# Differential attention in a two-layer diffusion backbone: units of two heads against units of one head with alternating score banks

## Chip, cores and metric

The program runs on one core of a Trainium2 chip, as one launch. The metric is the device time of that launch in microseconds (us).

## What is computed

Two layers over 256 latent tokens (x) and 256 context tokens, model width 1024, all in float32. Layer 0 mixes tokens by a Fourier transform and windowed attention and ends in a dense SwiGLU. Layer 1 has the differential attention that this case is about, and then a SwiGLU over 8 experts of which each token takes two. The reference, cut to the differential attention:

```python
def diff_attend(q, k, v, lam):                 # 8 heads, 2 maps c per head, d = 64, v has e = 128
    s = jnp.einsum('bqhcd,bkhcd->bhcqk', q, k).astype(jnp.float32) * (q.shape[-1] ** -0.5)
    p = jax.nn.softmax(s, axis=-1)
    w = p[:, :, 0] - lam * p[:, :, 1]
    return jnp.einsum('bhqk,bkhe->bqhe', w.astype(v.dtype), v)

# diff_mixer: keys and values are those of context and x together (512); queries those of x (2 tiles of 128)
ox = (rmsnorm(ox, subln_g) * (1.0 - lam_init)).reshape(B, L, D_MODEL) @ w_out
```

So a head has two softmax maps over the same 512 keys, the second is subtracted with a factor, and the output of each head (128 wide) is normalised by its own root mean square before the output projection.

## The kernel before

The code is written engine by engine, each engine's program in one function, with counting semaphores between them; every engine works strictly in the order of its own program. The sync queue (SP) loads weights, the POOL queue loads small tables and the rows of the modulation.

**Weights.** Until the experts, weights come in blocks of 1 MB into a ring of six slots (`WRAW`, line 127), in the order of `raw_order` (lines 389 to 394); a slot is refilled when its block of six places before has been used (lines 449 to 461). There are two kinds. A modulation block (`ada`, line 961) is multiplied straight from the slot, four matrix products into bank 7, 8 blocks to a group of rows; `ada_rows` (line 1503) adds the bias on VectorE once a group is complete, and POOL stores the rows (`store`, line 541). A projection block is split into a high part on ScalarE (`hi_upto`, line 613) and a low part on VectorE (`lo_upto`, line 1475), into rings of `SPL` = 3 buffers; the low part releases the slot. The output projection of the second attention has four such blocks, `B_DOUT` and the next three. In `raw_order` the modulation blocks 32 to 47, which belong to the time of this attention, are mixed with them: blocks 32 to 43, two output blocks, 44 to 47, two output blocks.

**Second attention.** PSUM has 8 banks of 128x512. Work goes in 8 groups g of one query tile t = g // 4 and two heads, so four score maps. Per group:

- TensorE, lines 1242 to 1265: two modulation blocks; the scores of group g+1, four products into banks 0 to 3 (`scores1`, line 1225), as soon as ScalarE has read the banks; then, when VectorE has combined the maps of g, eight transposes of 128x128 into banks 4 and 5; then, when ScalarE has copied these out, eight products with the values into bank 6.
- ScalarE, lines 825 to 848: copies banks 4 and 5 out to `PT1`; the exponentials of group g+1 (`exps1`, line 815), four instructions, each of which also sums its rows into `SUMS`; then copies the outputs from bank 6 and squares them with sums for the later normalisation.
- VectorE, lines 1745 to 1765: waits for the exponentials; reciprocal of the sums, times lambda, scales the two first maps, adds the two second maps scaled (`P1`); then the row maximum of group g+1 over banks 0 to 3 and its negation (`maxima1`, line 1732).

Three other jobs stand in these loops. At g = 5 VectorE normalises query tile 0 (`sub_norm`, line 1737), for which ScalarE takes a square root (line 846). At g = 3 and 7 VectorE adds the modulation rows (line 1759). At g = 6 and 7 output blocks 0 and 1 are split, ScalarE's part behind its squares (line 848), VectorE's behind its maximum (line 1762). Behind the loop come the normalisation of tile 1, the transposes of the output (line 1271), their high parts on ScalarE (line 853), the low part of output block 2 (line 1768) and the low parts of the output (line 1771), and then the output projection (line 1275).

**What follows.** SP loads the first expert blocks once all scores are issued (line 497) and their places are free. POOL waits for the last value product (line 598), then loads gate and norm rows. The expert stage (`experts`, line 1344) runs over 8 experts with a ring of 14 slots of 1 MB; SP refills a slot when TensorE has used it.

Of the kernel before, what the change touches and what calls it, by code (L numbers as in the profile page):

```python
# [75 lines left out]
SPLIT_AHEAD = 2  # L76
ADA_ATT0 = [3, 3, 2, 2, 2, 2, 2, 0]
# [39 lines left out]
def backbone(nc, x, c, ctx_in, c_ctx, ada_w, ada_b, norm_g, mix_in_w, mix_out_w, win_sink, diff_qkv_w,  # L117
# [111 lines left out]

    TRI, ROPE = T2[:, 0:256], T2[:, 256:448]  # L230
# [212 lines left out]
    def _(sp):  # L443
# [51 lines left out]
        def experts(rnd):  # L495
            if rnd == 0:
                sp.wait_ge(scores, 16)
# [35 lines left out]
    def _(pool):  # L533
# [49 lines left out]
        pool.wait_ge(pv_done, 8)  # L583
# [14 lines left out]
        pool.wait_ge(pv_done, 16)  # L598
# [11 lines left out]
    def _(act):  # L610
# [204 lines left out]
        def exps1(g):  # L815
            act.wait_ge(negmax, 8 + g + 1)
            if g:
                act.wait_ge(p_tr, 24 + 2 * g)
            for j in range(4):
                ins = act.activation(P1[:, j, :], ps[:, j, :], ACT.Exp, bias=NEGM[:, j:j + 1], scale=SCALE,  # L820
                                     accum_out=SUMS[:, j:j + 1])
            ins.then_inc(exps, 1)

        exps1(0)
        for g in range(8):
            t, hp = g // 4, g % 4
            act.wait_ge(p_tr, 24 + 2 * g + 1)
            act.wait_ge(pv_done, 8 + g)
            act.activation(PT1[:, 0:2, :], ps[:, 4, :].rearrange("p (c q) -> p c q", c=2),
                           ACT.Copy).then_inc(pt_even, 1)  # L830
            act.wait_ge(p_tr, 24 + 2 * g + 2)
            act.activation(PT1[:, 2:4, :], ps[:, 5, :].rearrange("p (c q) -> p c q", c=2),
                           ACT.Copy).then_inc(pt_odd, 1)
            if g < 7:
                exps1(g + 1)
            act.wait_ge(pv_done, 8 + g + 1)
            act.activation(OA[:, t, 256 * hp:256 * hp + 256], ps[:, 6, 0:256], ACT.Copy)
            if g:
                act.wait_ge(o_raw, g)
            for hh in range(2):  # L840
                n_ = t * 8 + 2 * hp + hh
                ins = act.activation(T2[:, P * hh:P * hh + P], ps[:, 6, P * hh:P * hh + P], ACT.Square,
                                     accum_out=SS[:, n_:n_ + 1])
            ins.then_inc(o_raw, 1)
            if g == 5:
                sqrt(0, 8)
            if g >= 6:
                hi_upto(B_DOUT + g - 5)
# [99 lines left out]
    def _(pe):  # L948
# [276 lines left out]
        def scores1(g):  # L1225

            t, hp = g // 4, g % 4
            if g:
                pe.wait_ge(exps, 8 + g)
            else:  # L1230
# [744 lines left out]
```

## Time and profile before

| | before |
|---|---|
| median of 3 runs | 1974.8 us (1969.48 to 1976.64) |
| profiled execution, its own time | 1977.56 us |
| span of the profile | 1975.8 us |
| TensorE matmuls busy | 1820.3 us (92%) |
| VectorE, ScalarE busy | 475.0 us (24%), 386.9 us (20%) |
| mean granted clock of TensorE | 0.952 of full |

A matmul in float32 is recorded as two instructions, so eight products show as x16. Almost all of TensorE's products are issued through one helper and so carry line 950; what they are is read from their operands: `work` alone are scores, `work,pt` are values, `w_raw,cond_stationary` are modulation blocks. Times in a timeline are microseconds from the span's start.

### The profile page before, as it was taken

How to read it: one execution, taken by the hardware profiler on the slowest of the kernel's cores; microseconds unless marked ns; L12 is line 12 of the kernel's file. 1: busy time of each engine (PE TensorE's matmuls, PEld its weight loads, DVE VectorE, ACT ScalarE, POOL GpSimd, SP SyncE). 2: the span in 40 equal slices, each digit the busy share in tenths (PEclk: the TensorE clock that was granted, in tenths of full speed). 3: DMA queues.
4: the chain of work that ended last, by engine and by line, in shares of the span. 5: the costliest groups of instructions: out<-in, count | busy, mean ns of one | idle time of the engine just before them, and what ended most of it. 6: DMA issues, size and time to landing. Idle time of an engine off the chain costs nothing. (4 is left out here: it accounts for less than half of the span.)

```text
span 1975.8 us, 35831 instructions
## 1 busy us (share of the span) xinstructions
PE 1820.3 (92%) x16214; PEld 1069.0 (54%) x16214; DVE 475.0 (24%) x762; ACT 386.9 (20%) x662; POOL 34.8 (2%) x71
## 2 busy tenths in 40 slices
PE   5999789999999889865799999999999999999995
PEld 2743478888888768544535345353443534435342
DVE  3313445222233663454310100101001010010103
ACT  3223433222232432342100000100001000010001
POOL 1000100000000000000000000000000000000000
PEclk8998899999999999987699999999999999999997
DMA  9255462332324232347599999999999999999970
GB/s 372 96 171 171 144 187 72 99 100 93 107 86 138 69 109 84 129 150 271 228 339 367 369 363 375 327 364 373 368 361 335 364 371 361 368 334 365 369 294 24
DMA packets 141160, 477.43 MB, mean 242 GB/s; under 512 B 11168, under 2 KB 35096, under 8 KB 122576
## 3 DMA queue, kind: packets, MB, share of 16 engines
q1 hardware_dynamic: 137344, 467.64, 64.5%
q0 software_dynamic: 3664, 7.48, 1.2%
q8 instruction: 129, 2.11, 0.4%
q14 instruction: 23, 0.19, 0.0%
HBM read 473.96 MB, written 1.13 MB: 240 GB/s over the span
## 5 line engine op out<-in xcount | busy, mean ns | idle before, releaser
L950 PE MATMUL ps<-w_hi,h_t 128*128 128x512 f32 (+1 forms) x960 | 298.2, 391 | 18.9 <-DVE h_t L1532 7.2
L950 PE MATMUL ps<-w_moe,h_te 128*32 128x256 f32 (+1 forms) x3520 | 296.6, 493 | 16.4 <-DVE residual L1876 16.4
L950 PE MATMUL ps<-h_t,w_hi 128*128 128x512 f32 (+1 forms) x768 | 222.5, 374 | 5.0 <-DVE h_t L1532 5.0
L950 PEld LDWEIGHTS ps<-w_moe,h_te 128*32 128x32 f32 x3520 | 113.2, 111 | 193.3 <-issue 138.9
L950 PE MATMUL ps<-w_raw,h_te 128*32 128x256 f32 (+2 forms) x3648 | 216.8, 396 | 0.0
L1479 DVE TENSOR_TENSOR w_lo<-w_raw,w_hi 128x2048 fp32r<-128x2048 f32 x58 | 132.9, 2292 | 349.0 <-ACT w_hi L619 348.5
L950 PEld LDWEIGHTS ps<-w_hi,h_t 128*128 128x128 f32 x960 | 182.6, 193 | 59.7 <-issue 8.3
L950 PE MATMUL ps<-w_lo,h_t 128*128 128x512 f32 (+1 forms) x480 | 186.9, 389 | 0.0
L1875 DVE TENSOR_TENSOR residual<-silu_g,ps 128x512 f32<-128x512 f32 (+1 forms) x32 | 19.8, 618 | 650.7 <-ACT silu_g L894 650.7
L619 ACT ACTIVATE w_hi<-w_raw 128x2048 fp32r<-128x2048 f32 x58 | 110.8, 1914 | 327.9 <-PE ps L950 319.4
L950 PEld LDWEIGHTS ps<-w_raw,h_te 128*32 128x32 f32 x3648 | 112.2, 110 | 100.9 <-issue 61.5
L950 PE MATMUL ps<-w_raw,work 128*32 128x512 f32 x1984 | 166.2, 487 | 0.0
L950 PEld LDWEIGHTS ps<-h_t,w_hi 128*128 128x128 f32 x768 | 141.9, 191 | 30.3 <-issue 5.6
L893 ACT ACTIVATE silu_g<-ps 128x512 f32<-128x512 f32 (+1 forms) x32 | 17.4, 544 | 655.1 <-PE ps L950 655.1
L950 PE MATMUL ps<-work 128*32 128x256 f32 (+6 forms) x752 | 137.7, 521 | 7.9 <-ACT p L820 4.9
L950 PE MATMUL ps<-h_t,w_lo 128*128 128x512 f32 (+1 forms) x384 | 143.6, 374 | 0.0
L950 PEld LDWEIGHTS ps<-w_raw,work 128*32 128x32 f32 x1984 | 62.0, 110 | 96.2 <-issue 77.1
L950 PEld LDWEIGHTS ps<-w_lo,h_t 128*128 128x128 f32 x480 | 92.7, 193 | 17.8
L950 PEld LDWEIGHTS ps<-work 128*32 128x32 f32 (+3 forms) x752 | 51.5, 135 | 75.1 <-issue 46.4
L950 PE MATMUL ps<-w_moe,work 128*32 128x512 f32 (+1 forms) x1088 | 91.0, 487 | 0.0
L950 PE MATMUL ps<-work,h_te 128*32 128x256 f32 (+1 forms) x1024 | 88.7, 493 | 1.0 <-ACT h_te L882 1.0
L950 PEld LDWEIGHTS ps<-h_t,w_lo 128*128 128x128 f32 x384 | 73.4, 191 | 12.6
(233 smaller groups left out, 1213.6 us busy)
## 6 DMA issues: line engine op xcount, KB each, us to landing
w_moe<-in_expert_in_w_dram SPq DMA_DIRECT2D x110, 1024.0 KB, 6.2
w_raw<-in_expert_out_w_dram SPq DMA_DIRECT2D x62, 1024.0 KB, 7.1
w_raw<-in_expert_in_w_dram SPq DMA_DIRECT2D x50, 1024.0 KB, 7.7
w_raw<-in_ada_w_dram SPq DMA_DIRECT2D x48, 1024.0 KB, 5.0
w_moe<-in_expert_out_w_dram SPq DMA_DIRECT2D x34, 1024.0 KB, 7.0
work<-in_expert_in_w_dram SPq DMA_DIRECT2D x32, 1024.0 KB, 7.2
w_raw<-in_expert_in_w_dram SPq DMA_DIRECT2D x64, 512.0 KB, 4.8
w_raw<-in_ffn_in_w_dram SPq DMA_DIRECT2D x44, 512.0 KB, 4.9
```

What stands on the lines that cost most here:

```text
L619: act.activation(WHI[:, b % SPL, :], WRAW[:, slot_w[b], :], ACT.Copy).then_inc(hi_done, 1)
L893: act.activation(SIL[:, 0:h], ps[:, 0, 0:h], ACT.Silu)
L950: return pe.matmul(out_, l, r, start=first, stop=last, skip_group_check=True)
L1479: dve.tensor_tensor(WLO[:, b % SPL, :], WRAW[:, slot_w[b], :], WHI[:, b % SPL, :].bitcast(F32), ALU.subtract).then_inc(lo_done, 1)
L1875: dve.tensor_tensor(ACTN[:, 0:h], SIL[:, 0:h], ps[:, 1, 0:h], ALU.mult)
```

## The change

The second attention goes in 16 units of one head and one query tile. Unit u has two score maps, in banks 0 and 1 for even u and 2 and 3 for odd u; its transposes go to bank 4 or 5, its copied maps to one half of `PT1` (`PT2` is a view of it), its output to bank 6. TensorE issues the scores of unit u+2 behind the transposes of unit u, and scores 0 and 1 ahead of the loop. The maps are combined without being normalised: map 0 minus map 1 times lambda times the ratio of their sums; ScalarE multiplies the output by the reciprocal of the first sum as it copies and as it squares. The modulation blocks go one to a unit. The first modulation rows are added at u = 8, the second behind the loop. Tile 0 is normalised by VectorE at u = 11, with ScalarE's root at u = 10. Output blocks 0, 1 and 2 are split at u = 13, 14 and 15. Counts that SP and POOL wait for follow the new number of units.

```diff
@@ -74,6 +74,10 @@
 assert EB % RING == 0 and len(ROUND) == NE * EB
 assert GROUP * 3 == CAP
 SPLIT_AHEAD = 2
+U0 = 8
+T0 = 24
+C0 = 12
+U1 = 16
 ADA_ATT0 = [3, 3, 2, 2, 2, 2, 2, 0]
 
 
@@ -227,6 +231,7 @@
     SPARE = work(6144, 2, BLK)
     MT = MODB[:, 0:1024].rearrange("p (g n) -> p g n", g=2)
 
+    PT2 = PT1.rearrange("p a b -> p (a b)").rearrange("p (u c q) -> p u c q", u=2, c=4)
     TRI, ROPE = T2[:, 0:256], T2[:, 256:448]
     UPPER, ONES, IOTA, IOTA8 = TM[:, 0:P], TM[:, P:2 * P], TM[:, 2 * P:3 * P], TM[:, 3 * P:3 * P + 16]
 
@@ -494,7 +499,7 @@
 
         def experts(rnd):
             if rnd == 0:
-                sp.wait_ge(scores, 16)
+                sp.wait_ge(scores, U0 + U1)
                 for n in range(RING):
                     if 2 <= n < 2 + RAW:
                         was, j = raw_order[N_RAW - RAW + n - 2]
@@ -580,7 +585,7 @@
         store(3)
         mod_rows(1)
         mod_rows(2)
-        pool.wait_ge(pv_done, 8)
+        pool.wait_ge(pv_done, U0)
         gate_rows(0)
         pool.wait_ge(used, B_FFNOUT + 5)
         gate_rows(1)
@@ -595,7 +600,7 @@
         store(5)
         for g in (4, 5):
             pool.wait_ge(mod_stored[g], 64)
-        pool.wait_ge(pv_done, 16)
+        pool.wait_ge(pv_done, U0 + U1)
         gate_rows(2)
         pool.dma_start(SCB, mod[1, 0:1, 4 * D:5 * D].broadcast_to([P, D])).then_inc(moe_in, 16)
         pool.dma_start(SHB, mod[1, 0:1, 3 * D:4 * D].broadcast_to([P, D])).then_inc(moe_in, 16)
@@ -812,40 +817,36 @@
 
         act.wait_ge(lam_dve, 1)
         act.activation(LAM[:, 2:4], LAM[:, 0:2], ACT.Exp).then_inc(lam_exp, 1)
-        def exps1(g):
-            act.wait_ge(negmax, 8 + g + 1)
-            if g:
-                act.wait_ge(p_tr, 24 + 2 * g)
-            for j in range(4):
+        def exps1(u):
+            p = 2 * (u % 2)
+            act.wait_ge(negmax, U0 + u + 1)
+            if u >= 2:
+                act.wait_ge(p_tr, T0 + u - 1)
+            for j in range(p, p + 2):
                 ins = act.activation(P1[:, j, :], ps[:, j, :], ACT.Exp, bias=NEGM[:, j:j + 1], scale=SCALE,
                                      accum_out=SUMS[:, j:j + 1])
             ins.then_inc(exps, 1)
 
         exps1(0)
-        for g in range(8):
-            t, hp = g // 4, g % 4
-            act.wait_ge(p_tr, 24 + 2 * g + 1)
-            act.wait_ge(pv_done, 8 + g)
-            act.activation(PT1[:, 0:2, :], ps[:, 4, :].rearrange("p (c q) -> p c q", c=2),
-                           ACT.Copy).then_inc(pt_even, 1)
-            act.wait_ge(p_tr, 24 + 2 * g + 2)
-            act.activation(PT1[:, 2:4, :], ps[:, 5, :].rearrange("p (c q) -> p c q", c=2),
-                           ACT.Copy).then_inc(pt_odd, 1)
-            if g < 7:
-                exps1(g + 1)
-            act.wait_ge(pv_done, 8 + g + 1)
-            act.activation(OA[:, t, 256 * hp:256 * hp + 256], ps[:, 6, 0:256], ACT.Copy)
-            if g:
-                act.wait_ge(o_raw, g)
-            for hh in range(2):
-                n_ = t * 8 + 2 * hp + hh
-                ins = act.activation(T2[:, P * hh:P * hh + P], ps[:, 6, P * hh:P * hh + P], ACT.Square,
-                                     accum_out=SS[:, n_:n_ + 1])
-            ins.then_inc(o_raw, 1)
-            if g == 5:
+        for u in range(U1):
+            t, h, p = u // 8, u % 8, u % 2
+            if u < U1 - 1:
+                exps1(u + 1)
+            act.wait_ge(p_tr, T0 + u + 1)
+            if u >= 2:
+                act.wait_ge(pv_done, U0 + u - 1)
+            act.activation(PT2[:, p, :, :], ps[:, 4 + p, :].rearrange("p (c q) -> p c q", c=4),
+                           ACT.Copy).then_inc(pt_even if p == 0 else pt_odd, 1)
+            act.wait_ge(pv_done, U0 + u + 1)
+            act.activation(OA[:, t, P * h:P * h + P], ps[:, 6, 0:P], ACT.Copy, scale=RL[:, 2 * p:2 * p + 1])
+            if u:
+                act.wait_ge(o_raw, u)
+            act.activation(T2[:, 0:P], ps[:, 6, 0:P], ACT.Square, scale=RL[:, 2 * p:2 * p + 1],
+                           accum_out=SS[:, u:u + 1]).then_inc(o_raw, 1)
+            if u == 10:
                 sqrt(0, 8)
-            if g >= 6:
-                hi_upto(B_DOUT + g - 5)
+            if u >= 13:
+                hi_upto(B_DOUT + u - 12)
         sqrt(8, 8)
         act.wait_ge(lam_dve, 2)
         for b in range(4):
@@ -1222,46 +1223,40 @@
             if n == 1:
                 nat_transposes(0)
 
-        def scores1(g):
-
-            t, hp = g // 4, g % 4
-            if g:
-                pe.wait_ge(exps, 8 + g)
-            else:
-                pe.wait_ge(nat_evac, 4)
-            for j in range(4):
-                h, p0 = 2 * hp + j // 2, HD * (j % 2)
-                ins = mm(ps[:, j, :], QT1[p0:p0 + HD, h, t * P:(t + 1) * P], KT1[p0:p0 + HD, h, :], True, True)
+        def scores1(u):
+
+            t, h, p = u // 8, u % 8, 2 * (u % 2)
+            if u >= 2:
+                pe.wait_ge(exps, U0 + u - 1)
+            for j in range(2):
+                ins = mm(ps[:, p + j, :], QT1[HD * j:HD * j + HD, h, t * P:(t + 1) * P],
+                         KT1[HD * j:HD * j + HD, h, :], True, True)
             ins.then_inc(scores, 1)
 
+        pe.wait_ge(nat_evac, 4)
         pe.wait_ge(v_even, 1)
         pe.wait_ge(v_odd, 1)
         scores1(0)
+        scores1(1)
         pe.wait_ge(v_even, 2)
         pe.wait_ge(v_odd, 2)
-        for g in range(8):
-            for a in range(4 * DK + 2 * g, 4 * DK + 2 * g + 2):
-                ada(a)
-            if g < 7:
-                scores1(g + 1)
-            pe.wait_ge(prob_scaled, 8 + g + 1)
-            for hb in range(2):
-                if g:
-                    pe.wait_ge(pt_even if hb == 0 else pt_odd, 12 + g)
-                for cc in range(2):
-                    for hh in range(2):
-                        o = ps[:, 4 + hb, cc * 256 + hh * P:cc * 256 + hh * P + P]
-                        ins = pe.transpose(o, P1[:, 2 * hh, (2 * hb + cc) * P:(2 * hb + cc + 1) * P], ID[:])
-                ins.then_inc(p_tr, 1)
-            if g:
-                pe.wait_ge(o_raw, g)
-            pe.wait_ge(pt_even, 12 + g + 1)
-            pe.wait_ge(pt_odd, 12 + g + 1)
-            for hh in range(2):
-                h = 2 * (g % 4) + hh
-                for c_ in range(4):
-                    ins = mm(ps[:, 6, hh * P:(hh + 1) * P], PT1[:, c_, hh * P:(hh + 1) * P],
-                             V1[:, c_, h * P:(h + 1) * P], c_ == 0, c_ == 3)
+        for u in range(U1):
+            h, p = u % 8, u % 2
+            ready = pt_even if p == 0 else pt_odd
+            pe.wait_ge(prob_scaled, U0 + u + 1)
+            if u >= 2:
+                pe.wait_ge(ready, C0 + u // 2)
+            for c_ in range(4):
+                ins = pe.transpose(ps[:, 4 + p, c_ * P:(c_ + 1) * P], P1[:, 2 * p, c_ * P:(c_ + 1) * P], ID[:])
+            ins.then_inc(p_tr, 1)
+            if u < U1 - 2:
+                scores1(u + 2)
+            ada(4 * DK + u)
+            if u:
+                pe.wait_ge(o_raw, u)
+            pe.wait_ge(ready, C0 + u // 2 + 1)
+            for c_ in range(4):
+                ins = mm(ps[:, 6, 0:P], PT2[:, p, c_, :], V1[:, c_, h * P:(h + 1) * P], c_ == 0, c_ == 3)
             ins.then_inc(pv_done, 1)
         pe.wait_ge(o_norm, 2)
         for b_ in range(4):
@@ -1729,10 +1724,11 @@
         dve.wait_ge(small_in, 32)
         link(dve.tensor_scalar(GSUB[:, 1:2], GSUB[:, 0:1], 1.0 - LAM_INIT, None, ALU.mult))
         dve.sem_inc(lam_dve, 1)
-        def maxima1(g):
-            dve.wait_ge(scores, 8 + g + 1)
-            link(dve.tensor_reduce(MX[:], ps[:, 0:4, :], AX_X, ALU.max))
-            dve.tensor_scalar(NEGM[:], MX[:], -SCALE, None, ALU.mult).then_inc(negmax, 1)
+        def maxima1(u):
+            p = 2 * (u % 2)
+            dve.wait_ge(scores, U0 + u + 1)
+            link(dve.tensor_reduce(MX[:, p:p + 2], ps[:, p:p + 2, :], AX_X, ALU.max))
+            dve.tensor_scalar(NEGM[:, p:p + 2], MX[:, p:p + 2], -SCALE, None, ALU.mult).then_inc(negmax, 1)
 
         def sub_norm(t):
 
@@ -1742,28 +1738,25 @@
             dve.tensor_tensor(o, o, r, ALU.mult).then_inc(o_norm, 1)
 
         maxima1(0)
-        for g in range(8):
-            dve.wait_ge(exps, 8 + g + 1)
-            link(dve.reciprocal(RL[:], SUMS[:]))
-            link(dve.tensor_scalar(NRL[:], RL[:], LAM[:, 0:1], None, ALU.mult))
-            for hh in range(2):
-                ins = dve.tensor_scalar(P1[:, 2 * hh, :], P1[:, 2 * hh, :], RL[:, 2 * hh:2 * hh + 1], None, ALU.mult)
-            link(ins)
-            for hh in range(2):
-                ins = dve.scalar_tensor_tensor(out=P1[:, 2 * hh, :], in0=P1[:, 2 * hh + 1, :],
-                                               scalar=NRL[:, 2 * hh + 1:2 * hh + 2], in1=P1[:, 2 * hh, :],
-                                               op0=ALU.mult, op1=ALU.add)
-            ins.then_inc(prob_scaled, 1)
-            if g < 7:
-                maxima1(g + 1)
-            if g in (3, 7):
-                ada_rows(4 if g == 3 else 5)
-            if g >= 6:
-                lo_upto(B_DOUT + g - 5)
-            if g == 5:
-                dve.wait_ge(o_raw, 4)
+        for u in range(U1):
+            p = 2 * (u % 2)
+            if u < U1 - 1:
+                maxima1(u + 1)
+            if u == 8:
+                ada_rows(4)
+            dve.wait_ge(exps, U0 + u + 1)
+            link(dve.reciprocal(RL[:, p:p + 2], SUMS[:, p:p + 2]))
+            link(dve.tensor_scalar(NRL[:, p:p + 1], RL[:, p + 1:p + 2], LAM[:, 0:1], SUMS[:, p:p + 1],
+                                   ALU.mult, ALU.mult))
+            dve.scalar_tensor_tensor(out=P1[:, p, :], in0=P1[:, p + 1, :], scalar=NRL[:, p:p + 1], in1=P1[:, p, :],
+                                     op0=ALU.mult, op1=ALU.add).then_inc(prob_scaled, 1)
+            if u >= 13:
+                lo_upto(B_DOUT + u - 12)
+            if u == 11:
+                dve.wait_ge(o_raw, 8)
                 sub_norm(0)
-        dve.wait_ge(o_raw, 8)
+        ada_rows(5)
+        dve.wait_ge(o_raw, U1)
         sub_norm(1)
         lo_upto(B_DOUT + SPL)
         for b in range(4):
```

## Rows read from the trace of the kernel before

**Rows 1.** One stretch of the expert stage: us, engines' busy time, granted clock, DMA.

```profile
core 0: us, PE busy (x) PEld busy (x) DVE busy (x) ACT busy (x) POOL busy (x), PEclk, DMA share, GB/s
...
1000.00:1100.00 100.00, 100.00 (x1297) 45.51 (x1298) 6.30 (x13) 6.64 (x16) 0.00 (x0) 1.00 0.97 360
```

**Rows 2.** Timeline, one group: start us, us, engine, line, operation, count, idle before.

```profile
848.98 2.28 DVE L1734 TENSOR_REDUCE row_max<-ps 128x4 f32<-128x2048 f32 x1
...
849.12 1.09 PE L1254 MATMUL ps<-ident,p 128*128 128x128 f32 x8 [0.35 <-DVE p L1753]
...
851.04 2.02 PE L950 MATMUL ps<-work,pt 128*128 128x128 f32 x16 [0.83 <-ACT pt L832]
...
851.30 0.17 DVE L1735 TENSOR_SCALAR neg_max<-row_max 128x4 f32<-128x4 f32 x1
...
853.00 1.92 PE L950 MATMUL ps<-w_raw,cond_stationary 128*32 128x512 f32 x16
...
854.32 0.18 DVE L1747 RECIPROCAL row_recip<-row_sums 128x4 f32<-128x4 f32 x1 [2.85 <-ACT p L820]
...
854.79 0.88 DVE L1750 TENSOR_SCALAR p<-p,row_recip 128x512 f32<-128x512 f32 x2
...
854.85 1.99 PE L950 MATMUL ps<-work 64*128 64x512 f32 x8
...
855.71 1.41 DVE L1753 SCALAR_TENSOR_TENSOR p<-p,row_recip_lam 128x512 f32<-128x512 f32 x2
...
857.04 2.28 DVE L1734 TENSOR_REDUCE row_max<-ps 128x4 f32<-128x2048 f32 x1
```

**Rows 3.** Line 1654, row maximum of the first attention: ns minimum, median, maximum.

```profile
L1654 DVE TENSOR_REDUCE row_max<-ps x8: 1224/1758/2292, 145.6 to 223.2; 128x4 f32<-128x2048 f32 x4, 128x4 f32<-128x1024 f32 x4
```

**Rows 4.** Timeline, end of group 6 and group 7.

```profile
877.07 1.95 ACT L619 ACTIVATE w_hi<-w_raw 128x2048 fp32r<-128x2048 f32 x1
...
881.25 0.17 DVE L1747 RECIPROCAL row_recip<-row_sums 128x4 f32<-128x4 f32 x1
...
884.11 1.97 PE L1254 MATMUL ps<-ident,p 128*128 128x128 f32 x8 [5.85 <-DVE p L1753]
...
886.86 3.63 PE L950 MATMUL ps<-work,pt 128*128 128x128 f32 x16 [0.78 <-ACT pt L832]
```

**Rows 5.** Timeline, start of the attention loop.

```profile
807.12 2.29 DVE L1734 TENSOR_REDUCE row_max<-ps 128x4 f32<-128x2048 f32 x1
...
812.48 3.78 PE L950 MATMUL ps<-work 64*128 64x512 f32 x8 [4.88 <-ACT p L820]
```

**Rows 6.** Timeline, from the last values to the first output product.

```profile
891.30 1.92 ACT L619 ACTIVATE w_hi<-w_raw 128x2048 fp32r<-128x2048 f32 x1
...
898.27 3.68 PE L1271 MATMUL ps<-ident,work 128*128 128x128 f32 x16 [7.79 <-DVE work L1742]
...
901.99 0.69 ACT L853 ACTIVATE z_t<-ps,subln_col 128x512 fp32r<-128x512 f32 x1 [0.17 <-PE ps L1271]
...
904.50 2.29 DVE L1479 TENSOR_TENSOR w_lo<-w_raw,w_hi 128x2048 fp32r<-128x2048 f32 x1 [6.29 <-ACT w_hi L619]
...
909.49 0.80 PE L950 MATMUL ps<-w_hi,z_t 128*128 128x512 f32 x1 [7.54 <-DVE z_t L1771]
```

**Rows 7.** Timeline, normalisation of query tile 0.

```profile
863.15 1.28 ACT L628 ACT_TABLE_LOAD   x1
...
864.69 0.20 DVE L1492 RECIPROCAL rstd<-std 128x8 f32<-128x8 f32 x1 [5.09 <-ACT std L628]
...
866.87 0.17 DVE L1747 RECIPROCAL row_recip<-row_sums 128x4 f32<-128x4 f32 x1
```

**Rows 8.** DMA issues: times, KB each, median us to landing.

```profile
work<-in_norm_g_dram POOLq DMA_DIRECT2D x4, 512.0 KB, 8.1
```

**Rows 9.** Timeline, the first row that takes up the gate rows.

```profile
921.63 1.22 DVE L1557 TENSOR_TENSOR post<-post 128x1024 f32<-128x1024 f32 x1
```

**Rows 10.** The attention loop, one stretch of 4 us: columns as in rows 1.

```profile
856.00:860.00 4.00, 2.83 (x20) 1.79 (x18) 3.56 (x5) 1.52 (x3) 0.00 (x0) 1.00 1.00 416
```

## The prediction, made before the change was run

> **What bounds the kernel now.** I first asked where a saving could be lost. In the expert stage the stretch from 1000 to 1100 us shows TensorE busy all 100 us at a granted clock of 1.00 (its higher level), so never short of data [rows 1]. So the 970 us behind the attention are set by TensorE, and whatever the attention gains or loses reaches the end one for one. A measurement of this kernel can tell about 0.5%, 10 us, from no change.
>
> The changed stage runs from the first row maximum at 807.12 to the end of the last value product, 890.49. The timeline of one group shows what sets its pace [rows 2]. A group takes 8.06 us (maximum at 848.98, next at 857.04). VectorE runs maximum and negation for 2.32 us, then waits; ScalarE's four exponentials fill 851.30 to 854.32, 3.02 us with the wake-up; VectorE's reciprocal, scaling and combination fill 854.32 to 857.04. These three in turn are the whole period: a ring of VectorE and ScalarE. TensorE has 1.09 for eight transposes, 2.02 for values, 1.92 for two modulation blocks and 1.99 for four score products: 7.02 us of the 8.06. So the room in the steady loop is 1.04 us per group at most, 8 us in all. The remaining loss is in three longer stops: the first group, the normalisation of query tile 0, and the splitting of output-weight blocks.
>
> **The new ring.** A unit is one head and tile, so two units stand for a group. TensorE's order is transposes(u), scores(u+2), one modulation block, values(u). VectorE's is maximum(u+1), then combination(u). Hence maximum(u+2) waits for scores(u+2), which stand behind transposes(u); combination(u+1) stands behind that maximum; transposes(u+1) wait for it. Two pairs of banks take ScalarE out of the ring, but put TensorE in. Its length, per unit:
> - transposes 0.55 (half of 1.09) and scores 1.00 (half of 1.99) [rows 2], wake-up 0.05;
> - maximum over 1024 elements: the first attention has that form, at 1.22 us, against 2.29 for 2048 [rows 3]; with 0.04 to the next start, 1.26;
> - negation to the next start: nothing to 0.24, the step of a linked small operation (854.32 to 854.79 holds two [rows 2]). It is not linked, I take 0.10;
> - combination. From the reciprocal at 881.25 to the transposes at 884.11 is 2.86 us [rows 4]. The change removes the two scalings, 0.92 (854.79 to 855.71), and one of two combinations, 0.66 (half of 855.71 to 857.04) [rows 2]. That leaves 1.28. The small multiply has a second pointer operand, which may add 0.1.
>
> Sum: 1.60 + 1.26 + 0.10 + 1.28 = 4.24 us, two units 8.48 against 8.06. TensorE's own work is 3.51 a unit, so it idles 0.73. ScalarE's exponentials of u+1 start as transposes(u) start and take about 1.5, while VectorE wants them 2.96 after that start: off the ring. The scalings removed (0.92 a group) and the shorter ScalarE part are thus eaten by 1.60 of TensorE per unit that stood beside other work before.
>
> **The start, saves about 4.9 us, half is lost in the cold clock.** Maximum 1.26 after 807.12, wake-up and two exponentials 1.65 (3.02 less two of 0.68), combination 1.28: transposes(0) at 811.31. Before, TensorE came back at 812.48, its scores took 3.78 instead of 1.99 and the transposes after them 1.97 instead of 1.09 [rows 2, 4, 5]: half clock. Unit 0 is therefore cold: 0.99 + 1.89 + 1.92 + 1.82 = 6.62, and transposes(1) start at 817.93.
>
> **The normalisation of tile 0.** Now at unit 11, ScalarE's square root at unit 10. ScalarE is through with unit 10 as transposes(11) start: 3.51 of TensorE and 0.75 of its own after transposes(10). (It took 0.81 from 890.49, the end of the last values, to 891.30 for a copy and two squares [rows 4, 6]; one square goes, a pointer scale comes into the two left; 0.55 to 0.81, I take 0.75.) From table load to reciprocal 1.54, from there to the next combination 2.18 [rows 7], then maximum(13) and combination(12), 2.64: 6.39 from transposes(11) to (12) instead of 4.24, plus 2.15. It cost 4.5 before (12.55 between reciprocals at 854.32 and 866.87 [rows 2, 7], against 8.06).
>
> The modulation rows at unit 8 now stand between maximum(9) and combination(8), on the ring; a 128x512 operation, plus 0.70. So transposes(13) start at 817.93 + 12 x 4.24 + 0.70 + 2.15 = 871.66.
>
> **The splits.** High part on ScalarE plus low part on VectorE take 4.18 us (877.07 to 881.25 [rows 4]), and VectorE's combination of the next unit is queued behind the low part. Before, one block was split inside the loop, one behind the last values, one behind the transposes of the output. Now blocks 0, 1 and 2 are split at units 13, 14 and 15.
> - Unit 13 to 14: 3.51 + 0.75 + 4.18, then maximum(15) 1.36 and combination(14) 1.28: 11.08.
> - TensorE idles over 7 us there and comes back at half clock, as after 880: transposes 1.97, values 3.63 [rows 4]. Unit 14 to 15: 0.99 + 1.92 + 1.82 = 4.73, + 0.75 + 4.18 + 1.28 = 10.94.
> - Tail: 4.73 + 0.75 + 4.18, the last modulation rows 0.70 (hidden before), and the second normalisation, 2.79 (891.30 to 898.27 is 6.97, less one split): 13.15 to the output transposes.
> - From these to the first output product was 11.22 us (898.27 to 909.49), because the low part of block 2, at 904.50, stood ahead of VectorE's four low parts of the output [rows 6]. That block is now done. The last high part ends at 902.68, 4.41 after the transposes' start; one low part 0.70 and 0.05 follow: 5.16, a saving of 6.06.
>
> The sum: 871.66 + 11.08 + 10.94 + 13.15 + 5.16 = 911.99, against 909.49: **2.5 us later**. Behind that nothing changes in work.
>
> **What is moved past queues.** Block 2's load waits for the low part of block 0, some 19 us before it is wanted, so it is off the path; block 3's follows the low part of block 1, somewhat sooner than now. The sync queue's expert loads are queued behind it, the seventh waits for split 2; all come a little sooner, and the experts are 80 us away. POOL's last store of modulation rows waits for rows that now stand behind split 2, at 904 (13.15 less 2.79 after transposes(15)), and its gate and norm rows are queued behind: some 6 us for store and issues, 8.1 for the slowest to land [rows 8] make 918. VectorE took them up at 921.63 [rows 9], with the shift at 924. Hidden by 6 us only; without that cover each us late costs one.
>
> **Rivals.**
> 1. *TensorE sets the pace*, 0.14. The skill speaks for it: the Trainium skill, Perfetto Trace Analysis, section Optimizing Tensor Performance, Matmuls, says that independent groups of matmuls should rotate through banks, so that emptying one overlaps filling the next. By that rule units would run at TensorE's sum. In the rows this is 3.51 a unit, 0.73 less, over 12 units 8.8 us: 6.3 us faster than now, 1968.5. Against it: the order on VectorE, above. For it: the maximum could find its scores ready if transposes start before I think. It passes 0.5% only if a stop goes too.
> 2. *The clock falls inside the loop*, 0.14, the slower side. Before, the clock held at 1.00 with gaps of 0.35 and 0.83 a group; the stretch 856 to 860 had TensorE busy 2.83 of 4.00 at 1.00 [rows 10]. Now there is a gap of 0.73 in every 4.24, and one of some 2.3 at unit 11. A cold unit is 6.62, 2.38 more; three such make the change slower by 0.5%, six make it 16.8 us slower (1991.6), all twelve 31 us (2006).
> 3. *My sum*, 0.72: 2.5 us slower. Its unknowns: negation and pointer 0.1 either way over 12 units, -1.2 to +2.5; 0.2 less on ScalarE three times; the clock at unit 12, up to +2.4; POOL's rows up to +3. So -2 to +10.
>
> The same page, section Optimizing Scalar/DVE Operations, holds that larger operations spare a cost per instruction. Here that is 0.15 us for a maximum in two halves (2 x 1.22 against 2.29 [rows 3]), and is in the sum.
>
> **Numbers.** The profiled execution took 1977.56 us with a span of 1975.8; the median of the runs is 1974.8, inside their scatter of 7. I put the +2.5 on the median: 1977.3. The range takes in rival 1 (1968.5, less scatter) and rival 2 up to five cold units: 1967 to 1989; outside it lies most of what is left of the clock's case. Faster by over 0.5%: 0.07, half of rival 1. Slower: 0.18, rival 2 and the far end of my sum. Else 0.75.
>
> **What would show it.** In the new profile transposes(u) should follow each other by 4.2 us, each maximum start right behind TensorE's scores, with VectorE waiting for TensorE and hardly for ScalarE. The two splits in the loop should show as gaps of 11 us, the first output product at about 912 with no split ahead of it. Units of 3.5 us would make rival 1 right; transposes at 0.99 between units 2 and 11, rival 2. I am wrong if the maximum does not wait for scores, or if the expert stage starts later than the output product's shift says.

## The result and the profile after

| | before | changed |
|---|---|---|
| median (9 runs each) | 1974.8 us | 1980.35 us (1978.1 to 1983.33) |
| ratio, 95% interval | | 1.0032 [1.0021, 1.0044] |
| profiled execution: its time, span | 1977.56, 1975.8 us | 1981.09, 1979.3 us |
| first row maximum | 807.12 | 804.91 |
| first output transposes | 898.27 | 907.41 |
| first output product | 909.49 | 912.65 |
| first maximum to first output product | 102.37 us | 107.74 us |

The change makes the kernel slower by 0.3%, 5.5 us, clear of the scatter and less than 0.5%. The last line of the table is the measure that the rest of this text uses: the first maximum starts 3.36 us behind the start of the first scores both before (803.76) and after (801.55), behind small operations of VectorE, but its own place lies anywhere from 803.7 to 808.7 us in the executions profiled here. From there to the first output product the changed kernel takes 5.37 us more, nearly the whole of the difference of the medians.

Timeline of one unit in the steady loop of the changed kernel (start, duration, engine, line). It answers to [rows 2]; line 1250 are transposes, 1730 is the maximum, 1748 to 1751 the combination, 838 ScalarE's copy of the transposed maps.

```profile
850.99 0.66 PE L1250 MATMUL ps<-ident,p 128*128 128x128 f32 x4 [0.61 <-DVE p L1751]
...
851.57 1.13 PE L951 MATMUL ps<-work 64*128 64x512 f32 x4
...
852.63 1.06 PE L951 MATMUL ps<-w_raw,cond_stationary 128*32 128x512 f32 x8
...
852.75 1.23 DVE L1730 TENSOR_REDUCE row_max<-ps 128x2 f32<-128x1024 f32 x1 [1.82 <-PE ps L951]
...
853.63 1.16 PE L951 MATMUL ps<-work,pt 128*128 128x128 f32 x8
...
854.09 0.16 DVE L1748 RECIPROCAL row_recip<-row_sums 128x2 f32<-128x2 f32 x1
...
854.59 0.75 DVE L1751 SCALAR_TENSOR_TENSOR p<-p,row_recip_lam 128x512 f32<-128x512 f32 x1
...
855.39 0.66 PE L1250 MATMUL ps<-ident,p 128*128 128x128 f32 x4 [0.61 <-DVE p L1751]
```

Transposes follow each other by 4.40 us, two units 8.81 against a group's 8.06. In the order of time: transposes at 850.99, scores at 851.57, the maximum at 852.75 with 1.82 us of waiting for TensorE written behind it, the combination at 854.09, the next transposes at 855.39 after a wait for VectorE. Neither engine is busy all the time, each waits for the other. Before, VectorE's waits in the loop ended with ScalarE's exponentials (2.85 us in front of the reciprocal [rows 2]); those waits are gone.

The start, and the normalisation of query tile 0, which answers to [rows 5] and [rows 7]:

```profile
804.91 1.23 DVE L1730 TENSOR_REDUCE row_max<-ps 128x2 f32<-128x1024 f32 x1
...
809.26 1.09 PE L1250 MATMUL ps<-ident,p 128*128 128x128 f32 x4 [5.73 <-DVE p L1751]
...
810.28 2.08 PE L951 MATMUL ps<-work 64*128 64x512 f32 x4
...
815.16 0.60 PE L1250 MATMUL ps<-ident,p 128*128 128x128 f32 x4
```

```profile
859.80 0.66 PE L1250 MATMUL ps<-ident,p 128*128 128x128 f32 x4 [0.61 <-DVE p L1751]
...
859.97 1.28 ACT L633 ACT_TABLE_LOAD   x1
...
864.86 1.55 PE L951 MATMUL ps<-work,pt 128*128 128x128 f32 x8 [2.35 <-ACT pt L838]
...
866.33 1.11 PE L1250 MATMUL ps<-ident,p 128*128 128x128 f32 x4
...
867.37 1.82 PE L951 MATMUL ps<-work 64*128 64x512 f32 x4
...
871.89 0.66 PE L1250 MATMUL ps<-ident,p 128*128 128x128 f32 x4 [0.61 <-DVE p L1751]
```

TensorE comes back after 5.73 us of idling at half clock (1.09 us for four transposes, 2.08 for two score products, against 0.66 and 1.13 in the loop). At unit 11 ScalarE loads the table for the root at 859.97, the values wait 2.35 us for its copy of the maps, and the transposes of unit 12 come 6.53 us after those of 11. They are cold: 1.11 us, and the scores 1.82.

The splits and the tail, which answer to [rows 4] and [rows 6]:

```profile
876.34 1.91 ACT L624 ACTIVATE w_hi<-w_raw 128x2048 fp32r<-128x2048 f32 x1
...
878.28 2.29 DVE L1474 TENSOR_TENSOR w_lo<-w_raw,w_hi 128x2048 fp32r<-128x2048 f32 x1 [6.44 <-ACT w_hi L624]
...
883.12 1.12 PE L1250 MATMUL ps<-ident,p 128*128 128x128 f32 x4 [7.43 <-DVE p L1751]
...
894.21 1.12 PE L1250 MATMUL ps<-ident,p 128*128 128x128 f32 x4 [6.10 <-DVE p L1751]
...
901.78 2.29 DVE L1474 TENSOR_TENSOR w_lo<-w_raw,w_hi 128x2048 fp32r<-128x2048 f32 x1 [7.62 <-ACT w_hi L624]
...
907.41 3.67 PE L1266 MATMUL ps<-ident,work 128*128 128x128 f32 x16 [8.21 <-DVE work L1738]
...
912.65 0.80 PE L951 MATMUL ps<-w_hi,z_t 128*128 128x512 f32 x1 [1.56 <-DVE z_t L1764]
```

VectorE waits 6.44 us for the high part of block 0, TensorE 7.43 us for the combination of unit 14. Units 13 and 14 take 11.23 and 11.09 us. Behind the output transposes no weight block is split ahead of the first product, and these 5.24 us were 11.22.

### The profile page after: what moved, and what is told of

It is laid out like the page before. It is cut to its first block and busy times, and to the rows that moved or that the text cites. A ratio compares the mean times of both kernels' runs of the same rounds, so it can differ in the third digit from the quotient of the medians.

```text
span 1979.3 us, 35882 instructions
## 1 busy us (share of the span) xinstructions
PE 1821.4 (92%) x16214; PEld 1064.2 (54%) x16214; DVE 474.4 (24%) x778; ACT 390.9 (20%) x670; POOL 35.0 (2%) x71
## 3 DMA queue, kind: packets, MB, share of 16 engines
HBM read 473.96 MB, written 1.13 MB: 240 GB/s over the span
```

## The experiments

Two theories were to be told apart from their rivals: that the steady unit is a ring through TensorE's scores and VectorE's maximum and combination, and that the splits cost what they do because a low part waits for a high part on ScalarE that is queued behind the unit's values. All runs in one table; each ratio is against runs of the kernel before on the same chip. A run's median is of 4 to 12 executions, and the runs come from four chips, on which the kernel before had medians of 1974.13 to 1976.68; so the stage and the ratios say more than a difference of two medians.

| run | first maximum to first output product, us | median, us | ratio to before, 95% interval |
|---|---|---|---|
| changed kernel | 107.74 | 1980.35 | 1.0032 [1.0021, 1.0044] |
| 1 scores first | 101.05 | 1972.68 | 0.9987 [0.9977, 0.9997] |
| 2 high parts early | 91.13 | 1963.16 | 0.9936 [0.9918, 0.9954] |
| 3 both | 85.45 | 1956.78 | 0.9916 [0.9893, 0.9939] |
| 4 maps scaled again | 113.97 | 1985.87 | 1.0048 [1.0032, 1.0064] |
| 5 before, unnormalised alone | 100.13 | 1971.94 | 0.9982 [0.9969, 0.9996] |
| 6 tile 0 normalised late | 105.69 | 1975.86 | 1.0013 [0.9999, 1.0026] |
| 7 all edits | 82.09 | 1952.73 | 0.9891 [0.9875, 0.9908] |
| 8 before, high parts early | 91.81 | 1963.95 | 0.9945 [0.9928, 0.9963] |
| 9 before, all that fits it | 85.04 | 1956.21 | 0.9897 [0.9881, 0.9914] |
| 10 as 7, again | 84.17 | 1953.33 | 0.9886 [0.9867, 0.9906] |
| 11 high parts earlier still | 83.35 | 1956.05 | 0.9901 [0.9883, 0.992] |

**1. Scores first.** TensorE's loop in the changed kernel:

```diff
+            if u < U1 - 2:
+                scores1(u + 2)
             pe.wait_ge(prob_scaled, U0 + u + 1)
...
             ins.then_inc(p_tr, 1)
-            if u < U1 - 2:
-                scores1(u + 2)
             ada(4 * DK + u)
```

> The changed kernel with one edit: TensorE issues the scores of unit u+2 ahead of the transposes of unit u instead of behind them. Theory (the ring of a unit runs through TensorE's scores, because VectorE's maximum of u+2 stands ahead of its combination of u+1): the maximum finds its scores ready, the unit falls from 4.41 us to TensorE's own sum of about 3.8, over some 12 units 7 us less than the changed kernel, so about 1973. Rival (ScalarE's exponentials or VectorE alone set the pace, the order on TensorE does not matter): units stay at 4.4 us, 1980.

```profile
832.62 1.13 PE L951 MATMUL ps<-work 64*128 64x512 f32 x4
...
833.68 0.66 PE L1252 MATMUL ps<-ident,p 128*128 128x128 f32 x4
...
833.80 1.23 DVE L1730 TENSOR_REDUCE row_max<-ps 128x2 f32<-128x1024 f32 x1 [1.26 <-PE ps L951]
...
834.27 1.06 PE L951 MATMUL ps<-w_raw,cond_stationary 128*32 128x512 f32 x8
...
835.42 1.13 PE L951 MATMUL ps<-work,pt 128*128 128x128 f32 x8
...
837.54 0.66 PE L1252 MATMUL ps<-ident,p 128*128 128x128 f32 x4
```

In this timeline the scores at 832.62 stand ahead of the transposes at 833.68, and no TensorE row has a wait: scores, transposes, modulation block, values, scores. The unit is 3.85 us, and all units from 1 to 10 are. The time fell by 6.7 us in the stage and 7.7 in the medians, as the theory said (7). The rival is out. The maximum still waits (1.26 us in the row at 833.80), but for scores that TensorE issues as fast as it can. In exchange unit 11 is longer, 8.27 us with 3.73 behind it against 6.53 and 5.56.

**2. High parts early.** ScalarE's loop in the changed kernel:

```diff
-            if u >= 13:
-                hi_upto(B_DOUT + u - 12)
+            if u >= 12:
+                hi_upto(B_DOUT + min(u, 14) - 11)
```

> The changed kernel with one edit: ScalarE takes the high parts of output blocks 0, 1, 2 at units 12, 13, 14 instead of 13, 14, 15; VectorE's low parts stay at 13, 14, 15. Theory (the 11 us gaps come from the low part waiting for a high part that ScalarE reaches only behind the unit's values and squares): the low part finds its high part ready and partly fills VectorE's wait for scores, units 13 and 14 take about 4.8 instead of 11.2 and 11.1, and the tail loses about 6.5 more, 19 us in all, so about 1961. Rival (the splits' own 4.2 us of work are the cost, wherever they stand): at most 4 us less, 1976; or block 2 lands too late and ScalarE waits for it, some 5 us given back.

```profile
864.26 1.13 PE L951 MATMUL ps<-work,pt 128*128 128x128 f32 x8 [2.34 <-ACT pt L838]
...
870.14 0.66 PE L1250 MATMUL ps<-ident,p 128*128 128x128 f32 x4 [0.61 <-DVE p L1751]
...
870.17 1.91 ACT L624 ACTIVATE w_hi<-w_raw 128x2048 fp32r<-128x2048 f32 x1
...
872.11 2.29 DVE L1474 TENSOR_TENSOR w_lo<-w_raw,w_hi 128x2048 fp32r<-128x2048 f32 x1 [2.03 <-ACT w_hi L624]
...
876.96 0.80 PE L1250 MATMUL ps<-ident,p 128*128 128x128 f32 x4 [1.78 <-DVE p L1751]
...
881.28 0.66 PE L1250 MATMUL ps<-ident,p 128*128 128x128 f32 x4
...
883.91 2.29 DVE L1474 TENSOR_TENSOR w_lo<-w_raw,w_hi 128x2048 fp32r<-128x2048 f32 x1 [2.69 <-ACT w_hi L624]
...
890.27 3.68 PE L1266 MATMUL ps<-ident,work 128*128 128x128 f32 x16 [4.63 <-DVE work L1738]
```

The gain is 16.6 us in the stage, 17.2 in the medians, of 19 expected; the rival's 4 is far off. The splits' work is all there, 1.91 and 2.29 us for each block, but units 13 and 14 take 6.82 and 4.32 instead of 11.23 and 11.09, and the tail from transposes 15 to the output transposes 8.99 instead of 13.20. What I missed: the high part of block 0 starts only with the transposes of unit 13 (870.17), because ScalarE reaches it behind the squares of unit 12, and so the low part still waited 2.03 us. The unit took 6.82, not 4.8, and the tail gained 4.2, not 6.5: the low part of block 2 waited 2.69 us for its high part in the same way. ScalarE's rows show no wait for a block. Unit 12 shortened too, from 5.56 to 4.41, because the clock did not fall there; no row shows that the edit had a part in it.

**3. Both edits.**

> The changed kernel with both edits that were tried alone: scores ahead of transposes, and high parts one unit earlier. Theory (the two losses lie in different stretches): they add, 7.7 and 17.2 us less than the changed kernel, about 1955. Rival (with units of 3.85 us VectorE and ScalarE no longer have room for the splits, or the weight blocks land too late): 1960 or more.

They add, to about 1 us: 6.7 and 16.6 in the stage would make 84.4, it was 85.45, and the median of 1956.78 is near the 1955 expected. The two losses are separate. A finer sum can't be drawn from one profile each: unit 0 alone took 5.67 us in run 1 and 4.19 here.

**4. Maps scaled again**, in VectorE's loop, with ScalarE's scales taken off:

```diff
-            link(dve.tensor_scalar(NRL[:, p:p + 1], RL[:, p + 1:p + 2], LAM[:, 0:1], SUMS[:, p:p + 1],
-                                   ALU.mult, ALU.mult))
+            link(dve.tensor_scalar(NRL[:, p:p + 1], RL[:, p + 1:p + 2], LAM[:, 0:1], None, ALU.mult))
+            link(dve.tensor_scalar(P1[:, p, :], P1[:, p, :], RL[:, p:p + 1], None, ALU.mult))
```

> The changed kernel with the maps normalised again: one scaling of the first map per unit on VectorE, no scale on ScalarE's output copy and square. Theory (VectorE's combination lies on the ring of every unit): the scaling's 0.48 us comes onto each of 15 units, 7 us more than the changed kernel, about 1987. Rival (the unit is bound by TensorE and the combination is hidden): no difference, 1980.

```profile
831.73 0.49 DVE L1750 TENSOR_SCALAR p<-p,row_recip 128x512 f32<-128x512 f32 x1
...
834.82 1.23 DVE L1730 TENSOR_REDUCE row_max<-ps 128x2 f32<-128x1024 f32 x1 [1.82 <-PE ps L951]
...
836.60 0.49 DVE L1750 TENSOR_SCALAR p<-p,row_recip 128x512 f32<-128x512 f32 x1
```

The scaling at 831.73 takes 0.49 us, the unit went from 4.41 to 4.87 (831.73 to the next, 836.60). All of it came through: VectorE's combination is on the ring, in a unit in which VectorE is idle for 1.82 us. The stage lost 6.2 us, the median 5.5, of 7 expected.

**5. The kernel before with the unnormalised combination alone** (a second buffer for the reciprocals, so that ScalarE can read one while the other is written; ScalarE copies the output in two scaled halves):

```diff
-            link(dve.tensor_scalar(NRL[:], RL[:], LAM[:, 0:1], None, ALU.mult))
-            for hh in range(2):
-                ins = dve.tensor_scalar(P1[:, 2 * hh, :], P1[:, 2 * hh, :], RL[:, 2 * hh:2 * hh + 1], None, ALU.mult)
+            for hh in range(2):
+                ins = dve.tensor_scalar(NRL[:, 2 * hh + 1:2 * hh + 2], R_[:, 2 * hh + 1:2 * hh + 2], LAM[:, 0:1],
+                                        SUMS[:, 2 * hh:2 * hh + 1], ALU.mult, ALU.mult)
```

> The kernel before with the unnormalised combination alone, groups of two heads kept: two scalings per group go, one small linked operation comes, ScalarE copies the output in two scaled halves. Theory (VectorE's part lies on the ring of 8.06 us): 0.7 us less per group, 5 us in 7 groups, about 1970. Rival (ScalarE's extra copy or TensorE holds the group): no difference, 1975.

```profile
831.08 0.18 DVE L1753 RECIPROCAL row_recip<-row_sums 128x4 f32<-128x4 f32 x1 [2.85 <-ACT p L821]
...
831.34 1.99 PE L955 MATMUL ps<-work 64*128 64x512 f32 x8
...
833.38 2.29 DVE L1739 TENSOR_REDUCE row_max<-ps 128x4 f32<-128x2048 f32 x1 [0.18 <-PE ps L955]
```

Groups take 7.65 us, 0.41 less than before and not 0.7, and from the last transposes to the output transposes it takes 14.73 instead of 14.16: the stage gained 2.2 us of 5 expected. The rows show what came in its place. The scores start at 831.34, when the exponentials are done, and take 1.99; the maximum now waits 0.18 us for them. With four maps in four banks the next scores can't start before the exponentials end, and with a shorter combination they are the longer way round.

**6. Tile 0 normalised behind the loop**, with one root over both tiles:

```diff
-            if u == 10:
-                sqrt(0, 8)
...
-        sqrt(8, 8)
+        sqrt(0, 16)
...
-            if u == 11:
-                dve.wait_ge(o_raw, 8)
-                sub_norm(0)
```

> The changed kernel with one edit: query tile 0 is normalised behind the loop together with tile 1 (one square root over 16 columns), not at units 10 and 11. Theory: units 11 and 12, which took 6.53 and 5.56, fall to 4.41 each (the second because the clock no longer falls), the tail takes one more multiplication of 1.2: 2.1 us less than the changed kernel, 1978. Rival (the stop was hidden by what follows, and the tail is the path): 1 to 2 us more, 1982.

Units 11 and 12 are 4.40 and 4.41, 3.3 us less, the tail 14.43 instead of 13.20, and so the stage is 2.05 us shorter, as expected. The median of 1975.86 is 4.5 less than that of the changed kernel, but from another chip; the ratios differ by 0.2%, and their intervals overlap. The expectation's rival is out.

**7. All edits.** To the three edits come two modulation blocks ahead of the loop:

```diff
+        ada(4 * DK)
+        ada(4 * DK + 1)
         for u in range(U1):
...
-            ada(4 * DK + u)
+            if u < U1 - 2:
+                ada(4 * DK + u + 2)
...
-            if u == 8:
+            if u == 6:
                 ada_rows(4)
```

> All three edits together, and two modulation blocks ahead of the loop, so that TensorE does not idle cold before unit 0; the blocks go two units ahead of their old place, their first rows are added at unit 6. Theory: 1955 from the two edits, less some 3 for the normalisation (its stop is 8.3 + 3.7 instead of 7.7 where scores go first, the tail pays 1.2), less about 3 for unit 0 at full clock and units 14 and 15 without a block: 1949. Rival (the loop is then bound elsewhere, the end of the attention is hidden by loads for the output projection or the experts): 1955.

82.09 us in the stage and 1952.73 in the median; it beats both kernels, by 1.1% the one before. That lies between the theory (1949) and its rival (1955). Of the two terms of 3 us, the normalisation's came: against run 3, units 11 and 12 take 4.4 us less and the tail 1.3 more. The clock's did not, unit 0 took 4.21 us against 4.19 in run 3: the two blocks did not keep the clock, TensorE still waited 2.49 us behind them for the first exponentials, and its scores then took 2.08 us.

**8. The kernel before with its high parts one group earlier.**

```diff
-            if g >= 6:
-                hi_upto(B_DOUT + g - 5)
+            if g >= 5:
+                hi_upto(B_DOUT + min(g, 6) - 4)
```

> The kernel before with one edit: ScalarE takes the high parts of output blocks 0 and 1 at groups 5 and 6 instead of 6 and 7; VectorE's low parts stay. Theory (the wait of the low part for the high part is the loss, in either kernel): group 6 falls from 14.4 us by about 2 (the low part's 2.2 stays on VectorE's ring, ScalarE's 1.9 leaves it) and the tail behind the last values by 4, since low part 1 no longer waits there: 6 us less than before, 1969. Rival (the gain belongs to the units of one head alone): no difference, 1974.

```profile
870.57 1.97 PE L1254 MATMUL ps<-ident,p 128*128 128x128 f32 x8 [4.85 <-DVE p L1753]
...
872.83 2.29 DVE L1479 TENSOR_TENSOR w_lo<-w_raw,w_hi 128x2048 fp32r<-128x2048 f32 x1
...
877.30 0.18 DVE L1747 RECIPROCAL row_recip<-row_sums 128x4 f32<-128x4 f32 x1 [2.19 <-ACT p L820]
...
880.17 1.09 PE L1254 MATMUL ps<-ident,p 128*128 128x128 f32 x8
...
880.72 2.28 DVE L1479 TENSOR_TENSOR w_lo<-w_raw,w_hi 128x2048 fp32r<-128x2048 f32 x1
```

10.6 us in the stage, more than the 6 expected. Group 6 fell from 14.38 to 9.60 us, since low part 0 at 872.83 fell into VectorE's wait for the exponentials, of which 2.19 us were still left behind it, and low part 1 at 880.72 ran beside TensorE's last transposes. The rival is out: this loss was in the kernel before too, about two thirds as large. Set beside run 2 it says more: with high parts early in both, the two kernels take 91.13 and 91.81 us, ratios 0.9936 and 0.9945. The 5.4 us by which the changed kernel is behind the one before are gone once the wait for the high parts is mended in both.

**9. The kernel before with edits 5, 6 and 8.** It asks what the units of one head are worth by themselves.

> The kernel before, groups of two heads kept, with every improvement that does not need the new units: unnormalised combination, high parts one group earlier, query tile 0 normalised behind the loop. It asks what the units of one head are worth by themselves. Theory: from first maximum to first output product 91.8 us with the early high parts, less 2.2 for the combination and some 3 for the normalisation, 86.6, against 82.1 of the kernel with all edits on new units; the time 1959, and the units of one head are worth 4 to 6 us once their scores stand ahead of the transposes. Rival (the units are worth nothing, their gain is in the other edits): 1953.

**10. The kernel of 7 again, on the same chip.**

> The kernel with all edits on the new units once more, on the same chip as the one above, for a direct comparison. Expected as before: 1953, 82 us from first maximum to first output product.

Run 9 took 85.04 us in the stage, where 86.6 were expected, run 10 took 84.17, where 82 were; medians 1956.21 and 1953.33; the ratios' intervals, [0.9881, 0.9914] and [0.9867, 0.9906], overlap. With everything else mended, units of one head are worth 1 to 3 us, or nothing that these runs can tell; 4 to 6 were expected. (The kernel of 7 and 10 also has its two blocks ahead of the loop, which run 9 has not.) The group of two heads runs at 7.65 us, two units with scores first at 7.70.

**11. High parts of blocks 0 and 1 at units 11 and 12, low parts at 12 and 13.**

> The kernel with all edits on the new units, with the high parts of output blocks 0 and 1 one unit earlier still (units 11 and 12; block 2 stays at 14, it lands too late for more) and their low parts at units 12 and 13. In the runs with the high part at unit 12, its 1.95 us still ended 2 us after VectorE was ready for the low part, and unit 13 took 6.44. Theory: VectorE waits no more for ScalarE, but ScalarE, with 1.95 more in a unit of 3.85 of which it has 1.1 free, becomes what a unit waits for; units 12 and 13 take some 4.9 each instead of 3.85 and 6.44, so about 0.5 us is won, and block 2 comes earlier: 82 to 83 us from first maximum to first output product, 1952. Rival (the wait alone was the loss): 2.6 us less, 80.5 us and 1950.

83.35 us, between runs 7 and 10, and 1956.05, where theory and rival had 1952 and 1950. Nothing was won; units 12 and 13 took 7.15 and 5.49 us, not 4.9 each. High and low part stood one unit apart as before, and so VectorE's low part waited again, 2.74 us at unit 12 and 1.40 at unit 13. Two units apart was not tried.

## Why the prediction was right

The forecast, 2.5 us slower, had the sign and the reasons; measured are 5.37 in the stage and 5.5 in the medians, within the -2 to +10 that I gave my sum. The whole range of 1967 to 1989 was wide, and that the time fell into it shows little; the steps show more. I had also put what a measurement can tell at 0.5%; nine runs of each kernel told 0.3%. Step by step, from the first maximum:

| step | predicted | measured |
|---|---|---|
| to transposes 0 | 4.19 | 4.35 |
| unit 0, cold | 6.62 | 5.90 |
| units 1 to 10, with the modulation rows | 43.10 | 44.64 |
| unit 11 | 6.39 | 6.53 |
| unit 12 | 4.24 | 5.56 |
| unit 13 | 11.08 | 11.23 |
| unit 14 | 10.94 | 11.09 |
| transposes 15 to output transposes | 13.15 | 13.20 |
| to the first output product | 5.16 | 5.24 |
| sum | 104.87 | 107.74 |

The sum is 2.87 us short: 1.54 in units 1 to 10, 1.32 in unit 12, 0.72 the other way in unit 0, and 0.73 in all the others together.

**The ring** was right. Run 1 takes scores off it and the unit falls to TensorE's sum; run 4 adds to the combination and the unit grows by as much. My size was 4.24 and it is 4.40. The mis-sized term is transposes and scores, 1.60 against 1.76 (850.99 to 852.75): I took half of eight transposes and of four products, and half of a run of products leaves out the end that the last one has in either case (four score products are recorded with 1.99 us, two with 1.13, not 1.00). Ten units make 1.5 us of it.

**The bound** from the other side held too: TensorE's own work in a unit, 3.51 by halving, is 3.85 in run 1. Rival 1, the rule of rotating banks from the Trainium skill (Perfetto Trace Analysis, section Optimizing Tensor Performance, Matmuls), would have given this; in the changed kernel the banks rotated and the rule did not come true, and it did in run 1, where TensorE issued the scores before its wait for VectorE. The bound is also the reason why the change could not win much: 8.06 us of a group against 7.70 of two units at best.

**The clock.** Rival 2 in its small form: one unit, 12, was cold and took 5.56 us against 4.41 of its neighbours, which I had in the range and not in the sum. In the steady loop the clock held at 1.00, with a gap of about 0.6 us in every unit. The cold unit 0 was shorter than I made it, by 0.72: the clock rose before the unit was over, and its values took 1.17 us instead of 1.82.

**The splits** cost what I worked out, to 0.15 us a unit, and so did the tail. POOL's late rows were hidden: its loads went out at 912.05 to 914.69, and VectorE took them up at 924.48 without a wait, behind a low part.

Where the gain went that the change seems made for: the unnormalised combination takes 0.92 us a group off VectorE, and alternating banks take ScalarE's exponentials off the ring. The first is worth 2.2 us in the old loop (run 5) and 6.2 in the new one (run 4). The second was given back at once, because in TensorE's order the next scores stood behind transposes that wait for VectorE. And the splits, placed at the ends of units of half the length, stopped the loop twice instead of once: without that (run 2) the new kernel is 0.6% faster than the one before, but so is the old one with its own high parts early (run 8, 0.55%).

What is not settled: how the 16.6 us of run 2 divide between waits and the clock. An estimate from rows: in the changed kernel transposes, block and values of units 14 and 15 took 1.12, 1.93 and 2.08 us, where unit 13 had 0.66, 1.07 and 1.16, so 2.24 more in each, and unit 12 was 1.15 longer; the clock is thus at most 5.6 us of the 16.6, and the larger part is waits. Open is also whether high parts two units ahead of their low parts win more.

## What to carry to other kernels

A second pair of buffers helps only if every engine's own order lets work on it start early: write down, for one round of the steady loop, what each engine's next instruction waits for, and follow the ring; here the move of one line on TensorE was worth 7 us, and without it the steady loop with double banks ran slower than with the single set (8.81 us against 8.06). A job with a first part on one engine and a second on another costs less if they are placed a round apart, and stops the loop if both stand at the end of the same round; look at such side jobs (17 us here, 11 in the kernel before) before the loop itself. When a group is halved, don't halve its measured times: each half keeps the fixed end of its last instruction, 0.16 us in 1.6 here.

## What the runs showed of the hardware that was not expected

The granted clock does not follow from the length of a gap alone. TensorE's gap at unit 11 was followed by a fall to a mean of 0.68 over 4 us in the changed kernel (2.35 us, ahead of 864.86) and left the clock at 1.00 in run 2 (2.34 us, ahead of 864.26, the first row of that run's timeline). The two stretches, changed kernel first, run 2 second, which is 0.6 us ahead there (864.86 against 864.26):

```profile
core 0: us, PE busy (x) PEld busy (x) DVE busy (x) ACT busy (x) POOL busy (x), PEclk, DMA share, GB/s
860.00:864.00 4.00, 2.51 (x16) 0.68 (x15) 2.33 (x7) 3.96 (x6) 0.00 (x0) 1.00 0.69 244
864.00:868.00 4.00, 3.14 (x14) 2.50 (x16) 2.17 (x5) 2.27 (x9) 0.00 (x0) 0.68 0.60 240
```

```profile
core 0: us, PE busy (x) PEld busy (x) DVE busy (x) ACT busy (x) POOL busy (x), PEclk, DMA share, GB/s
859.40:863.40 4.00, 2.51 (x16) 0.68 (x15) 2.33 (x7) 3.96 (x6) 0.00 (x0) 1.00 0.67 244
863.40:867.40 4.00, 2.80 (x20) 1.72 (x21) 2.17 (x5) 2.69 (x11) 0.00 (x0) 1.00 0.62 242
```

TensorE was busy 2.51 of 4.00 us in the first stretch of both kernels, with the same number of instructions; what it did just before the gap is no different, and the clock still went two ways. Why stays open. The same kernel did both as well. Runs 7 and 10 are one kernel, and TensorE had the same gap in front of the first scores inside the loop:

```profile
811.57 2.08 PE L949 MATMUL ps<-work 64*128 64x512 f32 x4 [2.49 <-ACT p L826]
```

```profile
807.31 1.13 PE L949 MATMUL ps<-work 64*128 64x512 f32 x4 [2.48 <-ACT p L826]
```

In run 7 (first row) the granted clock was 0.50 from 811.50 to 814.60. In run 10 it was still 0.98 from 807.30 to 809.20 and then 0.54 from 809.20 to 812.80. So unit 0 took 4.21 and 5.29 us, and unit 14 took 4.58 and 5.43. Such differences, some of which cancel, made 2.08 us in the stage; with one profile of each kernel a difference of 2 us in the stage needs the periods of its units or groups beside it, as in runs 5 and 6.
